# Seven products for eight in the gate projection, expert rows added onto the output by accumulating DMAs, deferred semaphore clears, and a sixth weight buffer

## The chip, the cores and the metric

One core of a Trainium2 chip. The metric is device time in microseconds of one execution of the whole kernel. The kernel before takes 1611.61 us, the median of three runs (1611.59 to 1613.59).

## The reference

One layer of a decoder block, 1024 tokens of width 1024, float32. A modulated RMSNorm of x, then one input projection whose columns feed an RWKV-7 time mixing, a latent attention, and two gates of 1024 channels each; the two branches are projected to 1024, weighted by the gates, summed, projected again and added to x. Then a second RMSNorm and a mixture of 32 experts, two per token:

```
h = modulate(rmsnorm(x, g_norm_mix), sh_m, sc_m)
z = h @ w_in                                  # z_rwkv, z_mla, z_gates (2 x 1024 columns)
gate_rwkv, gate_mla = split(sigmoid(z_gates))
x = x + gt_m * ((gate_rwkv * (y_rwkv @ w_branch[0]) + gate_mla * (y_mla @ w_branch[1])) @ w_out)
h = modulate(rmsnorm(x, g_norm_ffn), sh_f, sc_f)
for e in range(32):                           # combine[:, e] is 0 for all but two experts of a token
    out += combine[:, e] * ((silu(h @ w_e_gate[e]) * (h @ w_e_up[e])) @ w_e_down[e])
return x + gt_f * out
```

## The kernel before

Each engine runs its own program, written out by hand with semaphore waits; nothing is scheduled by a planner. The work is in five phases: norms and the latent projections, the low-rank parts of the time mixing, the time mixing itself, attention, and the last one, which holds the gates, the branch projections, the output projection, routing and the experts. `phase()` (L225) ends each with a block of its own in which GpSimd clears all semaphores of the phase one by one (L234), with a barrier of all engines behind it.

**Products in two parts.** A float32 product of full accuracy is made of three float32r matmuls (`three`, L341): every operand is split into a high part (ACT, `high_part`, L335) and a low part (DVE, `low_part`, L338), and high x high, high x low and low x high are summed in PSUM.

**Gates (L2118 to L2135).** A tile is 128 gate channels x 1024 tokens: 8 slices of K x 2 halves of the tokens x 3 matmuls of 512 columns = 48 matmuls. There are 16 tiles, 8 for each of the two gates, in a loop of the engines over i with both gates `br` in its body. SyncE loads the next weights (0.5 MB) when a tile's matmuls are done, ACT takes the sigmoid of a finished tile out of PSUM into `G` and splits the next weights, DVE makes their low part. The h of both operands lies split in `hs`; the first splits of h and of the weights are made in the attention phase (`SPLITS`, L1813).

**Branches and output (L2137 to L2197).** y of the time mixing is read back into `x1[:, 0:4]` and split while the gates run. y of the attention lies in `YTM` and is split only after the last gate tile, since its high part goes over the split h (ACT L2221, DVE L2276 into `v_lo7`). The branch tile of `b` has the 24 matmuls of the first branch, then the 24 of the second.

**Routing (L2655 to L2748).** DVE finds each token's two experts and their weights `top`, and builds one-hot tiles; 16 matmuls (L2509) turn them into `idx`, the token of each row of each pass, and `home`, the row number 0 to 2047 (token + 1024 for a token's second expert) to which the result goes.

**Experts (L2412 to L2653).** 24 fixed passes of 128 rows, 96 rows of room per expert, so 4 experts in 3 passes; then a loop over overflow passes. Per pass, GpSimd gathers the rows of h by an indirect DMA into one of three buffers `xg` (`fetch`), TensorE transposes them (L2520), multiplies by gate and up weights (L2542) and by the down weights (L2560); DVE multiplies the result by the FFN gate `gt` into one of four buffers `yo` (`rows_out`, L2768), and GpSimd sends these 128 rows by an indirect DMA to `y_dram`, 2048 rows (`send`, L2457). Unused rows carry an index out of bounds and move nothing. SyncE loads the experts' weights, 3 MB each, into five buffers: expert e goes out when the pass that last used expert e - 5 is through. GpSimd's order in the loop (L2468): wait for a free `xg`, gather, wait for `yo` of an earlier pass, send.

**Tail (L2782 to L2802).** When all sends have landed, SyncE reads the 2048 rows back in 16 DMAs, DVE adds each times `top` onto `x1` (L2789), and SyncE stores the 8 tiles of the output.

Of the kernel before, what the change touches and what calls it, by code (L numbers as in the profile page):

```python
# [15 lines left out]
P = 128  # L16
D = 1024
SEQ = 1024
KD = D // P
# [24 lines left out]
WB = 5  # L44
# [135 lines left out]
def build(nc, x, c, w_ada, b_ada, g_norm_mix, g_norm_ffn, w_decay_up, w_a_up, w_g_up, g_q_a, w_uq, g_kv_a,  # L180
# [6 lines left out]
    yr_dram = nc.dram_tensor("rwkv_rows", (P, CT * SEQ), f32, kind="Internal").ap()  # L187
    h2_dram = nc.dram_tensor("h2_rows", (SEQ, D), f32, kind="Internal").ap()
    y_dram = nc.dram_tensor("expert_rows", (2 * SEQ, D), f32, kind="Internal").ap()
    ctx = ExitStack()  # L190
    with ctx:
# [3 lines left out]
        taken = []  # L195
# [4 lines left out]
        r_in = [ctx.enter_context(nc.semaphore(f"r_in{i}")) for i in range(2 * NT)]  # L200
        w_in7 = [ctx.enter_context(nc.semaphore(f"w_in7{i}")) for i in range(2)]
        h_in7 = [ctx.enter_context(nc.semaphore(f"h_in7{i}")) for i in range(KD // PIECE)]
        mod_out = ctx.enter_context(nc.semaphore("mod_out"))
# [11 lines left out]
        def sem(st, name):  # L215
            taken.append(st.enter_context(nc.semaphore(name)))
            return taken[-1]
# [680 lines left out]
        with phase() as st:  # L898
# [14 lines left out]
            with nc.Block() as block:  # L913
# [11 lines left out]
                def _(pool):  # L925
                    nc.gpsimd.tensor_copy(crep2, csig[:].unsqueeze(2).broadcast_to([P, KD, 32])).then_inc(rep2_s, 1)
                    nc.gpsimd.memset(lw_pad[:, CT * SEQ:], 0.0)

# [91 lines left out]
        with phase() as st:  # L1020
# [91 lines left out]
            with nc.Block() as block:  # L1112
# [15 lines left out]
                def _(pool):  # L1128
# [53 lines left out]
                    for j in PERIODS:  # L1182
# [14 lines left out]
                        if step(n):  # L1197
                            inner_blocks(n)
                            outer_blocks(n, 0)

# [601 lines left out]
        with ExitStack() as st:  # L1802
            sb(st, "x1_place", [P, NT, D])
            sb(st, "G_place", [P, 2, KD, SEQ])
            hs = alias("hs", [P, 2, KD, SEQ])
            hraw = sb(st, "hraw", [P, 2, KD, SEQ])
            wh = alias("wh7", [P, 2, 1024])
            sb(st, "gt7_place", [P, 2, 1024])
            wl = alias("wl7", [P, 2, 1024])
            wraw = sb(st, "wraw7", [P, 2, 1024])  # L1810
        hh, hl = hs[:, 0], hs[:, 1]
        KLATE = 3
        SPLITS = [None, None] + list(range(KLATE, KD))  # L1813
# [3 lines left out]
        def gate_weights(sp, i, br):  # L1817
            src = w_gates[bass.ds(i + br * KD, 1)].rearrange("a p k n -> (a p) (k n)")
            sp.dma_start(wraw[:, br], src).then_inc(w_in7[br], 16)
# [1002 lines left out]
```

## Time and profile before

| what | value |
|---|---|
| median of 3 runs | 1611.61 us |
| profiled execution, its own time | 1609.88 us |
| its span, first to last instruction | 1608.0 us |
| mean granted TensorE clock | 0.941 of 2.4 GHz |
| TensorE matmuls busy | 1410.4 us, 14393 instructions |
| DVE / ACT / GpSimd busy | 700.8 / 470.3 / 258.6 us |
| moved by DMA | 238.07 MB |
| gate stage (from the first gate matmul to the first branch matmul) | 829 to 1004.5 us |
| expert passes (first gathered rows to the last send) | 1254.7 to 1568 us |
| tail (reading back, weighting, storing, clears) | 1568 to 1608 us |

The spans of the stages are read from the start times of their first and last instructions. Matmuls overlap: one of 512 columns is listed with 0.39 us, while the next one starts 0.225 us after it, so work on TensorE is counted by the pitch of the starts.

### The profile page before, as it was taken

To read this page: it belongs to the slowest core of one execution; us is meant where nothing else is said; L and a number is where in the kernel's file an instruction comes from. 1 tells how busy PE (TensorE), PEld (TensorE's weight loads), DVE (VectorE), ACT (ScalarE), POOL (GpSimd) and SP (SyncE) were. 2 spreads that over 40 slices of the span, in tenths; PEclk is the share of its full clock that TensorE was granted. 3 is DMA by queue.
4 is the path that set the end of the run, shared out by engine and by line. 5 is a ranking of instruction groups with operands and counts; after the bars stand their busy time and mean duration, and the time that the engine had idled before them with its cause. 6 is when DMAs were issued, how large, how long until landed. Compare 5 with 4: busy or idle time off the path is not lost. (4 is left out here: it accounts for less than half of the span.)

```text
span 1608.0 us, 32972 instructions
## 1 busy us (share of the span) xinstructions
PE 1410.4 (88%) x14393; PEld 1014.7 (63%) x14393; DVE 700.8 (44%) x990; ACT 470.3 (29%) x839; POOL 258.6 (16%) x301
## 2 busy tenths in 40 slices
PE   3799999965999988799889999998994899999980
PEld 0587777724899987577678888786883433333320
DVE  0645776746676755444641101555435212112124
ACT  1543232252343443444542222222111111111110
POOL 0001221205565551011110000000000111111110
PEclk8899999987999999799999999999996799999995
DMA  9831222260000020730011111313118599999947
GB/s 358 301 116 53 84 75 65 73 250 2 4 4 4 4 62 30 192 123 2 1 63 43 52 52 39 147 49 148 40 40 342 206 354 418 416 416 402 399 182 313
DMA packets 78759, 238.07 MB, mean 148 GB/s; under 512 B 8473, under 2 KB 41753, under 8 KB 61985
## 3 DMA queue, kind: packets, MB, share of 16 engines
q1 hardware_dynamic: 71280, 219.30, 36.9%
q0 software_dynamic: 7344, 16.79, 2.8%
q8 instruction: 108, 1.77, 0.4%
q14 instruction: 27, 0.21, 0.0%
HBM read 209.82 MB, written 36.19 MB: 153 GB/s over the span
## 5 line engine op out<-in xcount | busy, mean ns | idle before, releaser
L2542 PE MATMUL ps<-gu,xT 128*32 128x512 f32 x1536 | 176.5, 601 | 2.6 <-DMA gu<-w_e_up 2.0
L343 PE MATMUL ps<-hs,wh 128*128 128x512 f32 x320 | 125.9, 393 | 6.2 <-DVE v_lo L339 3.7
L345 PE MATMUL ps<-hs,wl 128*128 128x512 f32 x320 | 126.2, 394 | 0.0
L2542 PEld LDWEIGHTS ps<-gu,xT 128*32 128x32 f32 x1536 | 48.1, 111 | 108.3 <-issue 104.3
L2757 DVE TENSOR_TENSOR sg<-sg,ps 128x256 f32<-128x256 f32 x25 | 10.5, 422 | 213.4 <-ACT sg L2628 213.4
L344 PE MATMUL ps<-hs,wh 128*128 128x512 f32 x256 | 100.3, 392 | 0.0
L339 DVE TENSOR_TENSOR wl<-wraw,wh 128x1024 fp32r<-128x1024 f32 x24 | 29.4, 1225 | 150.5 <-ACT wh L336 150.5
L343 PE MATMUL ps<-hh,wr_h 128*128 128x512 f32 x224 | 93.1, 416 | 0.6 <-DVE wr_l L339 0.6
L344 PE MATMUL ps<-hl,wr_h 128*128 128x512 f32 x224 | 88.5, 395 | 0.0
L345 PE MATMUL ps<-hh,wr_l 128*128 128x512 f32 x224 | 88.4, 395 | 0.0
L2560 PE MATMUL ps<-dn,hidT 128*32 128x512 f32 x768 | 86.8, 592 | 0.5 <-ACT hidT L2632 0.5
L1996 DVE TENSOR_REDUCE nmax<-ps 128x1 f32<-128x896 f32 (+4 forms) x64 | 45.9, 753 | 71.7 <-PE ps L1895 71.1
L1392 DVE TENSOR_TENSOR inverses<-inverses,ps 128x512 f32<-128x512 f32 (+1 forms) x80 | 49.9, 631 | 61.5 <-PE ps L1615 61.1
L1178 POOL TENSOR_TENSOR off<-mats,cst 128x256 f32<-128x256 f32 x80 | 66.1, 845 | 53.4 <-PE ps L1599 53.3
L343 PEld LDWEIGHTS ps<-hs,wh 128*128 128x128 f32 x320 | 61.0, 191 | 20.0 <-DVE v_lo L339 4.1
L1615 PE MATMUL ps<-inverses,xx 64*64 64x64 f32 x1280 | 71.5, 218 | 0.2
L1890 PE MATMUL ps<-kT,qT 96*128 96x512 f32 (+3 forms) x160 | 63.6, 505 | 6.9 <-ACT causalr L1977 6.9
L345 PEld LDWEIGHTS ps<-hs,wl 128*128 128x128 f32 x320 | 60.9, 190 | 12.9
L2463 POOL MEMSET xg<- 128x3072 f32 x1 | 2.7, 2659 | 392.9 <-DVE YTM L2338 392.9
L1615 PEld LDWEIGHTS ps<-inverses,xx 64*64 64x64 f32 x1280 | 63.6, 135 | 0.4 <-issue 0.3
L1612 PE MATMUL ps<-xx,inverses 64*64 64x64 f32 x1024 | 63.3, 220 | 0.1
L487 POOL TENSOR_TENSOR qk<-qk,g_row 128x768 f32<-128x768 f32 x16 | 37.7, 2380 | 154.8 <-DVE qk L739 154.8
(366 smaller groups left out, 3018.5 us busy)
## 6 DMA issues: line engine op xcount, KB each, us to landing
gu<-w_e_gate SPq DMA_DIRECT2D x34, 1024.0 KB, 12.8
gu<-w_e_up SPq DMA_DIRECT2D x34, 1024.0 KB, 14.8
dn<-w_e_down SPq DMA_DIRECT2D x34, 1024.0 KB
wbuf<-w_ada SPq DMA_DIRECT2D x16, 1024.0 KB, 11.3
wbuf<-w_ada SPq DMA_DIRECT2D x16, 512.0 KB, 5.5
wraw<-w_gates SPq DMA_DIRECT2D x16, 512.0 KB, 3.3
rows<-expert_rows SPq DMA_DIRECT2D x16, 512.0 KB, 10.0
wr<-w_rwkv SPq DMA_DIRECT2D x14, 512.0 KB, 3.6
```

The source lines that it names most:

```text
L343: nc.tensor.matmul(out, wt[0], mov[0], start=(k == 0), stop=False)
L344: nc.tensor.matmul(out, wt[0], mov[1], start=False, stop=False)
L345: return nc.tensor.matmul(out, wt[1], mov[0], start=False, stop=(k == kn - 1))
L487: nc.gpsimd.tensor_tensor(rows, rows, g_row[:, i].unsqueeze(1).broadcast_to([P, HEADS, QKD]), ALU.mult).then_inc(gained, 1)
L1178: nc.gpsimd.tensor_tensor(off[:, g], mats[:, n % 2, 4 * g:4 * g + 4, 0], cst[:, a:a + CHUNK].unsqueeze(1).broadcast_to([P, 4, CHUNK]), ALU ...
L1392: nc.vector.tensor_tensor(now, now, add, ALU.add).then_inc(sm["t_ev"], 1)
L1612: nc.tensor.matmul(o[rows, 0:CHUNK], tt(j)[rows, hh, 1], xx[rows, hh], start=True, stop=True)
L1615: m = nc.tensor.matmul(o[rows, CHUNK:], xx[rows, hh], tt(j)[rows, hh, 1], start=True, stop=True)
L1890: nc.tensor.matmul(ps[:, 2 * (u % 2) + at // 512, at % 512:at % 512 + to - at], q, kT_[:, at - o * P:to - o * P], start=True, stop=True)
L1996: nc.vector.tensor_reduce(nmax[:, n:n + 1], score(u, i, o), AX.X, ALU.max, negate=True)\
L2542: last = nc.tensor.matmul(ps[part, GB[b]], xT[:, b, k, part], gu[:, expert(m, c_) % WB, :, k], start=(k == 0), stop=(k == KD - 1))
L2560: last = nc.tensor.matmul(ps[part, 6 + half], hidT[:, b, k, part], dn[:, expert(m, c_) % WB, k, half * 512:(half + 1) * 512], start=(k == ...
```

## The change

All four parts are in one diff.

**Clears.** The semaphores of a phase are held until the next phase is over, and GpSimd clears them there, in the middle of its own order. The block with its barrier is gone. Those of the last phase aren't cleared.

```diff
+        def clear_signals_of_last_phase(pool):
+            for s_ in before:
+                pool.sem_clear(s_)
...
             with ExitStack() as st:
                 yield st
-                with nc.Block() as block:
-                    @block.gpsimd
-                    def _(pool):
-                        for s_ in taken:
-                            pool.sem_clear(s_)
-                taken.clear()
+            held[1].close()
+            held.reverse()
+            before[:] = here
+            here.clear()
```

**Gates.** The tile i = 0 of both gates is made as before. For i = 1 to 7 the two tiles (2 x 128 channels by 1024 tokens, K = 1024) are taken as a 2 x 2 by 2 x 2 block product and made with seven block products (Strassen's scheme in Winograd's form). Each is 4 slices of K x 3 matmuls of 512 columns. The sums of h are made once at the start (T1, T2, T3 and one in place, 128x2048 each), the sums of the weights for each i. Products P1, P6, P7, P4 add up in one PSUM bank, out of which ACT copies the state after each of the first three; DVE adds the other banks. Loops of the engines over i are written out.

```diff
+            FACTORS = (A11, A21, S2, A12, S3, S4, A22)
+            P1, P5, P6, P2, P7, P3, P4 = range(7)
+            BANK = (0, 2, 0, 1, 0, 3, 0)
...
+                def product(i, j):
+                    pe.wait_ge(w_lo, number(i, j) + 2)
+                    if i == 1 and j in (P5, P6, P7, P4):
+                        pe.wait_ge(t_lo, (P5, P6, P7, P4).index(j) + 1)
+                    if j == P1 and i >= 2:
+                        pe.wait_ge(g_ev, evacuated(i - 2))
+                    if j in (P6, P7, P4):
+                        pe.wait_ge(ev_a, 3 * (i - 1) + (P6, P7, P4).index(j) + 1)
...
+                    for k in range(CT):
+                        cols = slice(k * P, (k + 1) * P)
+                        nc.tensor.matmul(out_t, hi[:, cols], mov_hi[:, k], start=(fresh and k == 0), stop=False,
+                                         skip_group_check=True)
+                        nc.tensor.matmul(out_t, hi[:, cols], mov_lo[:, k], start=False, stop=False,
+                                         skip_group_check=True)
+                        m = nc.tensor.matmul(out_t, lo[:, cols], mov_hi[:, k], start=False, stop=(k == CT - 1),
+                                             skip_group_check=True)
```

ACT splits product j's factor once product j - 2 is done (two buffers for high parts). The order of DVE within a step:

```diff
+                for i in range(1, KD):
+                    last = i == KD - 1
+                    if i > 1:
+                        factor_low(i, P5)
+                    factor_low(i, P6)
+                    factor_low(i, P2)
+                    if i == 1:
+                        sum_low(3)
+                    add(i, 0)
+                    factor_low(i, P7)
+                    add(i, 1)
+                    factor_low(i, P3)
+                    if last:
+                        y_low(0)
+                        y_low(1)
+                    factor_low(i, P4)
+                    add(i, 2)
+                    if last:
+                        y_low(2)
+                        y_low(3)
+                        weights(0, 7 * (KD - 1) + 2)
+                    else:
+                        for which in (SUM3, SUM1, SUM2):
+                            sums(i + 1, which)
+                        factor_low(i + 1, P1)
+                        sums(i + 1, SUM4)
+                    add(i, 3)
```

The sums need room: h is loaded a second time (4 MB) at the start of the phase, y of the time mixing is read back late, y of the attention is stored (2 MB) and read back. Both are split in four pieces each. The first branch products of both `b` now come before the second branch's, which alone wait for `v_lo`.

**Experts.** The routing matmuls carry a second half of columns (`block_is` has the token and its share, 84 columns for 42), which gives the share of each row; `home` is held twice, as it is and less 1024. The output tiles x1 are stored to `out` as they are made. Each pass's rows are multiplied by their share and the gate in one DVE operation, and are added onto `out` by two DMAs, one for the rows that are their token's first expert and one for the others; each waits until the one before it has landed.

```diff
+                def add(col, buf, done):
                     pool.indirect_dma_start(
-                        out=y_dram, out_offset=bass.IndirectOffsetOnAxis(ap=col.bitcast(u32), axis=0),
+                        out=out[0], out_offset=bass.IndirectOffsetOnAxis(ap=col.bitcast(u32), axis=0),
                         in_=yo[:, buf], in_offset=None,
-                        bounds_check=2 * SEQ - 1, oob_is_err=False).then_inc(y_out[buf], 16)
+                        bounds_check=SEQ - 1, oob_is_err=False, compute_op=ALU.add).then_inc(done, 16)
+
+                def add_first(j):
+                    pool.wait_ge(y_ev, 2 * j + 2)
+                    if j:
+                        pool.wait_ge(second_out, 16 * j)
...
+                    add(home[:, j, 0:1], j % YSLOTS, first_out)
+
+                def add_second(j):
+                    pool.wait_ge(first_out, 16 * j + 16)
+                    add(home[:, j, 1:2], j % YSLOTS, second_out)
...
                     fetch(idx[:, m:m + 1], m % XSLOTS)
-                    if m == XSLOTS:
-                        pool.wait_ge(home_s, 1)
-                    if m >= XSLOTS + 2:
-                        j = m - XSLOTS - 2
-                        pool.wait_ge(y_ev, 2 * j + 2)
-                        send(home[:, j:j + 1], j % YSLOTS)
+                    j = m - XSLOTS - 2
+                    if j >= 1:
+                        add_second(j - 1)
+                    if j >= 0:
+                        add_first(j)
...
-                        nc.vector.tensor_tensor(yo[:, buf, cols], ps[:, 6 + half], gt[:, cols], ALU.mult)\
-                          .then_inc(y_ev, 1)
+                        nc.vector.scalar_tensor_tensor(yo[:, buf, cols], ps[:, 6 + half], share_, gt[:, cols],
+                                                       ALU.mult, ALU.mult).then_inc(y_ev, 1)
+
+                def fixed_rows_out(m):
+                    if m >= YSLOTS:
+                        dve.wait_ge(second_out, 16 * (m - YSLOTS + 1))
+                    rows_out(m, m % YSLOTS, share[:, m:m + 1])
```

The tail (both blocks from L2782 to L2802) is gone. **WB = 6**: the sixth weight buffer and the FFN gate lie in the room of x1, so SyncE waits for the stores of x1 before it loads expert 5; it then goes out with experts 1 to 4, before the first pass.

## Rows read from the trace of the kernel before

**Rows 1.** The page: span, busy time by engine, GpSimd's DMA queue

```profile
span 1608.0 us, 32972 instructions
PE 1410.4 (88%) x14393; PEld 1014.7 (63%) x14393; DVE 700.8 (44%) x990; ACT 470.3 (29%) x839; POOL 258.6 (16%) x301
...
q0 software_dynamic: 7344, 16.79, 2.8%
```

**Rows 2.** Windows of four stages: length, busy by engine, clock, DMA share, GB/s

```profile
core 0: us, PE busy (x) PEld busy (x) DVE busy (x) ACT busy (x) POOL busy (x), PEclk, DMA share, GB/s
866.00:904.00 38.00, 38.00 (x169) 31.49 (x168) 4.90 (x4) 8.61 (x8) 0.00 (x0) 1.00 0.13 43
...
1222.00:1252.00 30.00, 12.51 (x53) 11.21 (x52) 21.79 (x60) 2.32 (x4) 0.91 (x1) 0.50 1.01 419
...
1344.00:1500.00 156.00, 154.05 (x1390) 55.35 (x1386) 28.96 (x53) 24.11 (x52) 26.40 (x26) 1.00 1.01 411
...
1568.00:1603.00 35.00, 0.00 (x0) 0.00 (x0) 20.01 (x16) 0.00 (x0) 0.00 (x0) 0.50 0.91 360
```

**Rows 3.** Chain of waits, routing and experts: start us, length us, what

```profile
1254.67 4.50 DMA xg<-h_rows,idx
...
1276.48 0.90 PE ps L2520 x8
...
1346.08 20.82 DMA gu<-w_e_up
...
1537.97 0.89 PE ps L2520 x8
```

**Rows 4.** Groups by shape in the gate stage, 830 to 1004 us, DVE and ACT

```profile
L339 DVE TENSOR_TENSOR wl<-wraw,wh 128x1024 fp32r<-128x1024 f32 x15 | 18.4, 1226 | 135.6 <-ACT wh L336 135.6
L339 DVE TENSOR_TENSOR yr<-x,yr 128x4096 fp32r<-128x4096 f32 x1 | 4.4, 4426 | 7.7 <-ACT yr L336 7.7
...
L2213 ACT ACTIVATE G<-ps 128x1024 f32 x14 | 14.4, 1028 | 45.2 <-PE ps L345 45.1
```

**Rows 5.** Waits, 828 to 1014 us: total, times, longest

```profile
PE ps L343 <- DVE v_lo L339: 3.7, 1, 3.7
```

**Rows 6.** Groups by shape in the expert stage, 1284 to 1500 us, DVE and ACT

```profile
L2768 DVE TENSOR_TENSOR YTM<-ps,gt 128x512 f32<-128x512 f32 x37 | 25.6, 692 | 27.1 <-PE ps L2560 27.1
...
L2623 ACT ACTIVATE xT<-ps 128x512 f32<-128x512 f32 x36 | 19.6, 595 | 2.2
```

**Rows 7.** Line L234, whole span, then 325 to 340, then from 1600 us

```profile
L234 POOLq EVENT_SEMAPHORE_RANGE_CLEAR  x244: 37/38/47, 329.1 to 1607.3; - x122
...
L234 POOLq EVENT_SEMAPHORE_RANGE_CLEAR  x79: 37/38/47, 329.1 to 334.5; - x79
...
L234 POOLq EVENT_SEMAPHORE_RANGE_CLEAR  x73: 37/38/43, 1602.7 to 1607.3; - x73
```

**Rows 8.** Chain of waits, last expert rows and tail

```profile
1563.87 0.70 DVE YTM L2768
1564.70 0.50 issue
1565.43 2.61 DMA expert_rows<-YTM,now
...
1592.80 1.28 DVE x L2789
```

**Rows 9.** Groups by shape in routing, 1230 to 1256 us

```profile
L2509 PE MATMUL ps<-block_is,row_is 128*128 128x42 f32 x32 | 7.1, 420 | 7.9 <-DVE row_is L2731 7.9
...
L2501 PE MATMUL ps<-each,rt 128*128 128x256 f32 x2 | 1.2, 715 | 8.9 <-DVE each L2690 8.9
...
L2729 DVE SCALAR_TENSOR_TENSOR block_is<-rt,block_is 128x336 f32<-128x336 f32 x2 | 1.0, 508 | 0.1
```

**Rows 10.** Line L2458: 1286 to 1516 us, then 1547 to 1549, then 1565 to 1567

```profile
L2458 POOL DMA_INDIRECT expert_rows<-YTM,home x20: 1002/1011/1016, 1286.0 to 1512.1; - x20
...
DMA to landing us min/median/max: 8.4/9.1/10.1
...
DMA to landing us min/median/max: 4.1/4.1/4.1
...
DMA to landing us min/median/max: 2.6/2.6/2.6
```

More of the change, by code:

```diff
@@ L193, in sb @@
             return st.enter_context(nc.sbuf_tensor(name, shape, dt))
-        taken = []
+        here, before = [], []
+        held = [ctx.enter_context(ExitStack()) for _ in range(2)]
         gu_in = [ctx.enter_context(nc.semaphore(f"gu_in{i}")) for i in range(WB)]
@@ new lines, in _, with branch_part @@
+                for br in range(2):
+                    whole_gate(br)
+                for i in range(1, KD):
+                    for j in range(7):
+                        product(i, j)
+                def branch_part(i, b, br):
+                    mov = ((yh, yl), (None, v_lo7))[br]
+                    for n in range(2):
+                        at = slice(n * 512, (n + 1) * 512)
+                        for k in range(CT):
+                            cols = slice((br * CT + k) * P, (br * CT + k + 1) * P)
+                            high = vh(k)[:, n] if br else mov[0][:, k, at]
+                            m = three(ps[:, 4 * b + 2 * br + n], (wh[:, b, cols], wl[:, b, cols]), (high, mov[1][:, k, at]),
+                                      k, CT)
+                    m.then_inc(b_mm, 1)
@@ L2218, in _, with factor_high @@
-                for br in range(2):
-                    gate(KD - 1, br)
-                    if br:
-                        high_part(vh, YTM[:]).then_inc(v_hi, 1)
-                    weights(br, KD * 16 + 16)
+                def factor_high(i, j):
+                    act.wait_ge(g_mm, max(1, 1 + number(i, j)))
+                    sums = {P5: SUM1, P6: SUM2, P7: SUM3, P3: SUM4}
+                    if j in sums:
+                        act.wait_ge(s_sum, 4 * (i - 1) + sums[j])
+                    else:
+                        act.wait_ge(w_in7[i % 2][FACTORS[j][0]], 16 * (i // 2 + 1))
+                    high_part(factor_hi(i, j), factor(i, j)).then_inc(w_hi, 1)
@@ L2224, in merged @@
+                gates(KD - 1)
+                weights(1, KD * 8 + 16)
+                for k in range(CT):
+                    v_high(k)
                 def merged(i):
@@ new lines, in y_low, with v_low @@
+                def y_low(k):
+                    dve.wait_ge(y_hi, k + 1)
+                    low_part(yl[:, k], x1[:, k], yh[:, k]).then_inc(y_lo, 1)
+                def v_low(k):
+                    dve.wait_ge(v_hi, k + 1)
+                    low_part(in_halves(v_lo7[:, k]), in_halves(YTM[:, k]), vh(k)).then_inc(v_lo, 1)
+                for which in (SUM3, SUM1, SUM2, SUM4):
+                    sums(1, which)
+                dve.wait_ge(raw_in[0], 16)
+                nc.vector.tensor_tensor(T1[:, 0], h12, h11, ALU.subtract).then_inc(t_sum, 1)
@@ L2280, in merge @@
+                weights(1, 7 * (KD - 1) + 3)
+                for k in range(CT):
+                    v_low(k)
+                def merge(i, b, ready=None):
                     m = 2 * i + b
@@ L2572, in gate_up @@
                             part = slice(UNIT * b, UNIT * (b + 1))
[L2573 removed]
+                            last = nc.tensor.matmul(ps[part, GB[0]], xT[:, 0, k, part], gu[OVER_W[b]][:, :, k],
                                                     start=(k == 0), stop=(k == KD - 1))
```

489 lines of the change are left out of this document (321 added, 168 removed).

## The prediction

> **What bounds the kernel now.** I read the page first: in 1608.0 us of span TensorE is busy 1410.4, DVE 700.8, and GpSimd's DMA queue carries 16.8 MB, half of it gathered rows and half sent ones [rows 1]. Then the windows by stage [rows 2]. In the gate stage, 866 to 904 us, TensorE is full at clock 1.00 (2.4 GHz) with 169 matmuls in 38 us, so one every 0.225 us; DVE does 4.9 of the 38, DMA is at 0.13. In the expert stage, 1344 to 1500, TensorE is busy 154 of 156 us and the DMA share is 1.01 at 411 GB/s: two resources are full at once. From 1568 to 1603 TensorE does nothing and the DMA engines move 360 GB/s: the tail. The chain of waits [rows 3] says the same: transposes of one expert pass follow the last by 11.76 us at best, from 1276.48 to 1537.97 are 22 passes in 261.5 us, 11.89 each, and in between stand a few pieces of "DMA gu<-w_e_up" that waited in a queue for 20 us. So any matmul less in the gate stage counts in full, everything after 1568 counts in full, and in the expert stage nothing may be slowed that sits on the DMA engines.
>
> **Part 1, seven products for eight.** The 16 gate tiles have 48 matmuls each. The first two stay; in each of the seven steps behind them 96 become 7 x 12 = 84. 7 x 12 matmuls less at 0.225 us [rows 2] = 18.9 us off TensorE. What is new: per step DVE has 4 sums, 7 low parts and 4 additions out of PSUM, each 128x512. The nearest row is 0.69 us for 128x512 out of PSUM [rows 6]: 15 x 0.69 = 10.4 us. ACT has 7 high parts, 3 copies at 0.60 each [rows 6] and 2048 columns of sigmoids, 1.03 per 1024 [rows 4]: 8.1 us. A step is 84 x 0.225 = 18.9 us, so both fit as sums. The order is tighter: from the end of P7 to the next step's P1 TensorE has two products, 5.4 us, while ACT copies and splits (1.2) and DVE has six operations in a row (low part of P4, addition, three sums, low part of P1: 4.1) with hand-overs of 0.3: 5.6. That is 0.2 us per step, 1.5 in all. At the start DVE must do four low parts of 1024 columns, six operations of 512, and seven of 2048 (1.23 us per 1024 [rows 4]; 4.43 for 4096 gives 2.2 to 2.45): 4.9 + 4.1 + 16.3 = 25.3 us, and waits some 2 us for the new loads, before it can split P6's factor; TensorE is there after 96 + 24 matmuls, 27 us. DVE starts a microsecond later than TensorE, so P6 comes 3.7 us late (bounds 0 and 8). At the end TensorE now waits 3.7 us for v_lo [rows 5]; with the second branch in pieces and 48 matmuls (10.8 us) ahead of it, this goes, but the pieces of y are in ACT's and DVE's order ahead of the first branch weights: four high and low parts plus one split after P7, some 1.7 us late. Part 1: -18.9 + 1.5 + 3.7 - 3.7 + 1.7 = -15.7 us.
> The added transfers (4 MB of h at the start, 4 MB of reloads, 2 MB stored) fall where the DMA share is 0.13 [rows 2]; their cover is some 20 us of matmuls each.
>
> **Part 2, the clears.** GpSimd clears 244 semaphores one by one, 73 of them after the last transfer [rows 7]. They take 0.065 us each (1602.7 to 1607.3 for the last 73) and every engine waits at a barrier: 244 x 0.065 = 15.9 us. They move into GpSimd's order beside other work (171 are left, the longest lot 79, 5.1 us, in stages where GpSimd has hardly any work) and the last 73 vanish. With them go five barriers; from the last clear, 1607.3, to the end of the span there are 0.7 us [rows 1, 7], and with one of two barriers left I take 0.3 us each, an estimate. -17.4 us.
>
> **Part 3, the tail.** Now the last send lands at 1565.43 + 2.61 = 1568.0 [rows 8], then 16 reads, 16 additions of 1.28 and 8 stores follow, up to 1602.7, where the clears begin [rows 7]. All of it goes: -34.7 us. The stores of x1 move into the output stage, one of 0.5 MB per tile of rows; nothing waits for them but SyncE, ahead of the sixth buffer.
>
> **Part 4, routing and first rows.** Two DVE operations of 336 elements (0.51 each) come ahead of the matmuls of L2509, and these have 84 columns for 42: +1.0 and, between 0 and 1.9 (42 more columns at the 1.4 ns per column between 0.42 us for 42 and 0.71 for 256 [rows 9]), I take +1.0. With the sixth buffer SyncE queues experts 1 to 5 and two stores, 16.8 MB, from 1221.5 on; at 419 GB/s [rows 2] that ends at 1261.6, where it ended at 1252. The first gather took 4.50 us beside little else [rows 3]; issued behind queued weights GpSimd's DMAs take 8.4 or more [rows 10]. Queue half gone by then: +3 us. Part 4: +5 us.
>
> **Part 5, the accumulating DMAs.** This decides the sign. For each pass the one send becomes two additions into the output, and no addition may start before the last has landed. The trace has no such DMA; the nearest rows are the sends. While weights stream, 20 sends land after 8.4 to 10.1 us, median 9.1; without weights one took 4.1 and the small last one 2.6 [rows 10]. From DVE's end to the DMA's start there are 0.86 us (1564.57 to 1565.43 [rows 8]). An addition carries half of a pass's rows, so I take the low end under load, 8.4 + 0.8 = 9.2, and without weights 3.2, between 2.6 and 4.1, + 0.8 = 4.0. Two under load make 18.4 us per pass against 11.89: the chain of additions becomes what sets the pace, and with four output buffers DVE and TensorE soon wait for it. That in turn leaves the DMA engines idle at times, where additions are fast. The account over the stage: from the first rows out (1285) 27 experts of 3.15 MB and 7 of the 8.4 MB of gathered rows remain, 92 MB; at 411 GB/s [rows 2] 224 us, and 10 more for the additions' own bytes in that time: 234 us under load. In these fit 234 / 9.2 = 25.4 additions; the other 22.6 take 4.0 each, 90 us. Chain: 324 us, from 1285.1 to 1609.4. Behind it the overflow pass: copies on GpSimd, two products with the gate on DVE (1.4), two additions of 2.6 + 0.86, in all some 9.5 us: 1618.8 in place of 1568.0, **+50.8 us**. The bounds: +3.5 (the additions stay within 11.89 us per pass and only the last pass has a second one, 0.86 + 2.6), and 48 x 9.9 = 475 us, which is +202.
> The waits ahead of each addition stand in GpSimd's order ahead of the next gather; three gather buffers and four output buffers cover that until the chain is the pace, and then the gather is early. The sixth buffer itself removes at most the 2 us by which TensorE waits for weights; beside a slower pace it is worth nothing.
> An addition reads the row it changes. If that doubles its bytes, 42 rows or 0.17 MB per DMA, 0.42 us, come on top: 48 x 0.42 + 6 = 26 us more. The Trainium skill (Collectives: The Full Stack, "The bandwidth ceiling: the fold count and why AG ≠ RS ≠ AR") says exactly this: an add in the DMA path needs two source reads on one ring and so runs at half a copy's rate. By that rule the sum would be 1626; no run here shows it yet, and I hold the copy's price because the landing under load hardly is a matter of bytes (the same 9 us for all 20 sends).
>
> **Sum.** 1608.0 - 15.7 - 17.4 - 34.7 + 5.0 + 50.8 = 1596.0 us of span; the profiled execution is 1.9 above its span, 1609.88, so 1597.9. The median of the runs is 1611.61, 1.7 above that execution: **1600 us**, 0.7% faster.
>
> **Rivals.**
> A, the forecast, 1600, own range 1580 to 1622. For it: landings of 9 us with the DMA engines full. Chance 0.40.
> B, the additions hide: two of them within a pass, a mean of 5.9 us or less with hand-over. Then 1600 - 50.8 + 3.5 = 1553. For it: an addition has half the rows, and sends of 4 us exist. Against: all 20 beside weights took 8.4 or more. Chance 0.22.
> C, slower: the chain of additions at the GpSimd queue is the pace all through, at a mean of 8 us per addition: 48 x 8 = 384, 60 us more than A, 1660. It decides against the change from a mean of 7.0 us on (336 us of chain eat all that parts 1 to 4 bring); A has 6.75, so the point is near. Chance 0.16.
> D, the seven products save nothing, because ACT's and DVE's order keeps TensorE waiting at each product: 1616. Each product has 2.7 us, and a split needs 1.4 to 2.3 of them. Chance 0.10.
> E, the row read as well as written counts double: 1626. Chance 0.12.
>
> **How the numbers follow.** A measurement of this kernel can tell 0.2%, 3.2 us, from no change, so faster means below 1608.4. A gives 0.30 faster, 0.04 same, 0.06 slower; B 0.22 faster; C 0.16 slower; D 0.04, 0.03, 0.03; E 0.01, 0.02, 0.09. Sum: 0.57, 0.09, 0.34. The range takes in B's 1553 and most of C: 1545 to 1655.
>
> **What would show it.** Part 1: gate steps of about 19 us, TensorE waits on DVE near their start only. Part 2: no stop of all engines for 79 clears at 329 [rows 7]. Part 3: no TensorE-free stretch of 35 us. Part 5: in the expert stage, transposes 13 to 14 us apart in place of 11.76, GpSimd and DVE waiting for the additions' landings, a DMA share well under 1, additions landing after 8 to 9 us beside weights and 3 to 4 alone. It is wrong if the passes keep 11.8 us (B), or if additions take over 8 us even where the DMA share is low (C).

## The result, and the profile after

The changed kernel takes 1695.47 us (median of 4 runs, 1690.71 to 1698.15) beside 1612.6 us for the kernel before on the same chip: ratio 1.0513, interval 1.0487 to 1.0539, so 5.1% slower. The forecast was 1600 us, range 1545 to 1655. The side is wrong and the time lies outside the range. It came out on the side of rival C (slower, the chain of additions as the pace), 35 us above C's 1660. The profiled execution took 1693.2 us, 1.9 of it outside its span.

The page of the changed kernel:

```profile
span 1691.3 us, 32837 instructions
PE 1418.3 (84%) x14309; PEld 1006.0 (59%) x14309; DVE 752.1 (44%) x1083; ACT 496.9 (29%) x906; POOL 312.5 (18%) x327
...
q0 software_dynamic: 10944, 16.82, 4.7%
...
DMA 23%; PE 22%; DVE 3%; issue 2%; ACT 1%; SPq 0%; POOLq 0%; POOL 0%; DVEq 0%
...
L2729 POOL DMA_INDIRECT out<-YTM,home x48 | 75.1, 1565 | 301.8 <-DMA out<-YTM,home 228.2
```

Against [rows 1] the span is 83.3 us longer. TensorE has 84 matmuls fewer, and 273.0 us of the span without work where it had 197.6. Just under a quarter of the chain that ended last is DMA, and the last row says whose: GpSimd issued 48 additions and waited 228 us for the landing of the one before. GpSimd's queue carries the same 16.8 MB as before, but its packets took 4.7% of the engines' time in place of 2.8%.

Windows of the changed kernel by stage (columns as in [rows 2]):

```profile
core 0: us, PE busy (x) PEld busy (x) DVE busy (x) ACT busy (x) POOL busy (x), PEclk, DMA share, GB/s
855.00:985.00 130.00, 130.00 (x563) 106.56 (x561) 68.12 (x102) 55.73 (x89) 0.00 (x0) 0.99 0.22 76
1280.00:1340.00 60.00, 59.93 (x540) 21.52 (x532) 11.72 (x20) 9.30 (x21) 11.06 (x8) 1.00 0.97 372
1340.00:1500.00 160.00, 117.22 (x928) 41.46 (x932) 20.60 (x36) 17.28 (x36) 37.80 (x27) 0.84 0.80 285
...
1600.00:1660.00 60.00, 27.48 (x216) 8.78 (x208) 6.95 (x12) 3.00 (x7) 18.17 (x12) 0.75 0.19 27
```

The gate stage is full with the seven products, at half of DVE's and under half of ACT's time. The expert stage is the new thing. Up to 1340 TensorE is full: four output buffers still hold what the additions have not taken away. From 1340 to 1500 it is busy 117 of 160 us, the DMA share is 0.80 where it was 1.01 [rows 2], and neither resource is the bound any more. From 1600 to 1660 no weights are left to load (27 GB/s). TensorE is full there up to 1628; then its work is done but for the overflow pass's last products, and it stands 40.5 us, until 1668.5, while the last additions go out one by one.

The chain of waits of the changed kernel (start us, length us, what):

```profile
1231.25 8.98 DMA xg<-h_rows,idx
...
1266.30 0.82 issue
1267.12 10.08 DMA out<-YTM,home
...
1277.25 0.76 issue
1278.01 9.88 DMA out<-YTM,home
...
1658.43 4.38 DMA out<-YTM,home
...
1666.22 2.20 DMA xg<-h_rows,now
...
1671.68 5.06 PE ps L2878 x16
...
1678.39 4.50 DMA out<-YTM,now
```

From 1267.12 on the pattern is landing, hand-over, landing, hand-over (the hand-over is the time from a landing to the start of the next addition). The first piece answers to the 4.50 us gather of [rows 3]. The last ones belong to the overflow pass. The gather that starts only at 1666.22 brings the rows of the block behind it; their transposes stand in TensorE's order ahead of the overflow pass's down product (5.06 us).

Line L2729 of the changed kernel, the additions, first over the whole span, then from 1267 to 1345 us (weights streaming), then from 1610 to 1660 us (none left):

```profile
L2729 POOL DMA_INDIRECT out<-YTM,home x48: 1551/1552/1609, 1267.1 to 1663.6; - x48
...
L2729 POOL DMA_INDIRECT out<-YTM,home x8: 1551/1579/1609, 1267.1 to 1343.1; - x8
...
DMA to landing us min/median/max: 8.9/10.0/10.8
...
L2729 POOL DMA_INDIRECT out<-YTM,home x9: 1551/1552/1552, 1613.1 to 1658.4; - x9
...
DMA to landing us min/median/max: 3.9/4.6/5.4
```

The last two groups hold the two prices that the forecast had to guess. It took 8.4 and 3.2 us; they are 10.0 and 4.6. Issuing one costs GpSimd 1.55 us where a send cost 1.01 [rows 10].

Waits from 1231 to 1691 us (total, times, longest):

```profile
POOL out L2729 <- DMA out<-YTM,home: 228.2, 39, 9.7
...
PE ps L2812 <- DMA xg<-h_rows,idx: 80.0, 11, 10.7
POOL out L2729 <- DVE YTM L3062: 70.7, 8, 10.4
...
PE ps L2812 <- DMA xg<-h_rows,now: 40.5, 1, 40.5
```

Two of these need care. TensorE waits 80 us for gathered rows, which looks like slow gathers; it is a symptom, because a gather is issued by GpSimd and stands in its order behind an addition that waits for a landing (experiments 5 and 6 settle that). And the 70.7 us that GpSimd waited "for DVE": 17.0 us of them are true: the first addition (7.0) and the first of the overflow pass (10.0) had only DVE's rows to wait for. The other six are not. In the chain such an addition starts 0.04 us after the end of DVE's operation, 0.83 us after the last landing. All 47 additions of the fixed passes behind the first follow the last landing by 0.76 to 0.87 us, but for two (1.14 and 1.55), so the landing held these too; the two events nearly coincide, since DVE was itself held up by the buffer that this landing set free.

**The time, stretch by stretch.** Kernels with the same program up to the first gather issue it anywhere from 1227.2 to 1237.0 us in their profiles, so single positions are good to a few microseconds; I compare durations. From the first matmul of the gate stage to the first gather: 412.3 us (818.91 to 1231.25), before 425.8 (828.89 to 1254.67). A little of this difference belongs to the clears: in the first 5.1 us of the stretch the kernel before has a granted clock of 0.67 and 15 matmuls, the changed kernel 1.00 and 22, and with the clears alone moved (experiment 1) the clock is 1.00 there too. From the gather to the first rows out: 35.9 us, before 31.3. From there to the end of the span: 424.2 us, before 322.0, and in those 322.0 the tail and the last clears (40.0 us) were included. So the whole loss, and more, lies behind the first rows out.

### The profile page after: what moved, and what is told of

Its sections match the earlier page's. It is cut to its first block, busy times and chain, and to the rows that moved or that the text cites. A ratio compares the mean times of both kernels' runs of the same rounds, so it can differ in the third digit from the quotient of the medians.

```text
span 1691.3 us, 32837 instructions
## 1 busy us (share of the span) xinstructions
PE 1418.3 (84%) x14309; PEld 1006.0 (59%) x14309; DVE 752.1 (44%) x1083; ACT 496.9 (29%) x906; POOL 312.5 (18%) x327
## 3 DMA queue, kind: packets, MB, share of 16 engines
q0 software_dynamic: 10944, 16.82, 4.7%
HBM read 207.73 MB, written 51.40 MB: 153 GB/s over the span
## 4 chain that ended last, share of the span: by engine, by line
DMA 23%; PE 22%; DVE 3%; issue 2%; ACT 1%; SPq 0%; POOLq 0%; POOL 0%; DVEq 0%
DMA out<-YTM,home 21%; PE ps L350 3%; PE ps L351 3%; PE ps L352 3%; PE ps L2229 3%; PE ps L2231 3%; PE ps L2233 3%; PE ps L2834 1%; DMA br<-b_router 1%; PE ps L2284 1%; PE ps L2275 1%; DMA xg<-h_rows,idx 1%; PE ps L2800 0%; PE ps L2812 0%; DVE YTM L3062 0%
## 5 line engine op out<-in xcount | busy, mean ns | idle before, releaser
L2834 PE MATMUL ps<-gu,xT 128*32 128x512 f32 x1296 | 188.8, 637 | 0.7 <-ACT xT L2915 0.7
L3053 DVE TENSOR_TENSOR sg<-sg,ps 128x256 f32<-128x256 f32 x25 | 10.5, 422 | 297.4 <-ACT sg L2920 297.4
L2812 PE MATMUL ps<-cst,xg 128*128 128x128 f32 x208 | 37.9, 341 | 120.5 <-DMA xg<-h_rows,idx 80.0
L2729 POOL DMA_INDIRECT out<-YTM,home x48 | 75.1, 1565 | 301.8 <-DMA out<-YTM,home 228.2
L2812 PEld LDWEIGHTS ps<-cst,xg 128*128 128x128 f32 x208 | 32.1, 205 | 124.4 <-DMA xg<-h_rows,idx 82.1
L2915 ACT ACTIVATE xT<-ps 128x512 f32<-128x512 f32 x52 | 29.4, 596 | 160.8 <-PE ps L2812 159.4
L2834 PE MATMUL ps<-gu_last,xT 128*32 128x512 f32 x240 | 62.6, 635 | 0.0
L350 PE MATMUL ps<-hs,M 128*128 128x512 f32 x144 | 57.9, 402 | 1.6 <-DVE hs L346 1.6
## 6 DMA issues: line engine op xcount, KB each, us to landing
gu<-w_e_gate SPq DMA_DIRECT2D x29, 1024.0 KB, 10.5
```

The costliest lines, as they stand in the source:

```text
L350: nc.tensor.matmul(out, wt[0], mov[0], start=(k == 0), stop=False)
L2729: pool.indirect_dma_start(out=out[0], out_offset=bass.IndirectOffsetOnAxis(ap=col.bitcast(u32), axis=0), in_=yo[:, buf], in_offset=None, b ...
L2812: last = nc.tensor.transpose(ps[:, g, j * P:(j + 1) * P], rows[:, 4 * g + j], C("ident"))
L2834: last = nc.tensor.matmul(ps[part, GB[b]], xT[:, b, k, part], gu[expert(m, c_) % WB][:, :, k], start=(k == 0), stop=(k == KD - 1))
```

## Experiments

Experiments 3 to 6 are one run each, all others medians of four; experiment 6 was run four times more as the last of 9 to 11.

**1. The clears alone.** The kernel before, with each stage's semaphores cleared by GpSimd inside a later stage:

```
-                with nc.Block() as block:
-                    @block.gpsimd
-                    def _(pool):
-                        for s_ in taken:
-                            pool.sem_clear(s_)
-                taken.clear()
+            held[1].close()
+            held.reverse()
+            before[:] = here
+            here.clear()
...
+                    clear_signals_of_last_phase(pool)
```

> The kernel before with the deferred clears alone. If all engines wait for the 244 clears and the barriers behind them, it saves 17.4 us: 1595 us. If other work (a transfer, a first load of the next phase) ends just as late, it saves less, 8 to 12 us: 1601 to 1605.

Measured: 1591.0 us against 1610.38, ratio 0.9891 (0.9867 to 0.9915). That is 19.4 us less; the forecast's part 2 was 17.4. Its span is 1588.9.

**2. Clears and seven products.** The same with the gate and branch part of the change; experts, sends, five weight buffers and the tail as before:

```
-        wh = alias("wh7", [P, 2, 1024])
+        small_r = alias("small_r", [P, 5, 512])
...
+        FACTORS = (A11, A21, S2, A12, S3, S4, A22)
+        P1, P5, P6, P2, P7, P3, P4 = range(7)
...
+                def product(i, j):
```

> The kernel before with the clears and the seven products, experts, sends, five buffers and tail as before. With 13.6 us for the seven products (18.9 less matmuls, 5 of waits at the start and at the end) on top of 17.4 for the clears: 1581 to 1583 us. If ACT's and DVE's order holds TensorE up at each product, no better than the clears alone: 1595.

Measured: 1575.31 us, ratio 0.979 (0.9774 to 0.9806), 15.7 us below experiment 1. Part 1 had said 15.7; for this run I had expected 13.6 and 1581 to 1583, and it lies below that. The agreement with part 1 to the tenth is luck: the four runs of this kernel lie between 1572.62 and 1578.00 us, those of experiment 1 between 1589.37 and 1596.80. The wait for P6's split is 7.3 us here and 6.6 in the changed kernel, where I had 3.7; against that, of the waits that I had put within the steps and at the end of the stage (1.5 and 1.7 us) TensorE has 0.5 us here and 1.0 in the changed kernel. This kernel computes all of the reference and beats both kernels of the case. Its expert stage shows what a full one looks like (window, columns as above):

```profile
1340.00:1500.00 160.00, 159.15 (x1436) 57.55 (x1432) 28.95 (x52) 25.90 (x56) 25.37 (x25) 1.00 1.00 408
```

So 1575 to 1695, 120 us, is what the new way out of the expert stage costs, with the shares in the routing and the sixth buffer in it (118 us by the two ratios, since the two kernels ran on different chips), though it saves the tail of 34.7 us.

**3. The same DMAs without the addition.** The changed kernel; the two DMAs of a pass overwrite rows of the output in place of adding to them, in the same order with the same waits:

```
                         in_=yo[:, buf], in_offset=None,
-                        bounds_check=SEQ - 1, oob_is_err=False, compute_op=ALU.add).then_inc(done, 16)
+                        bounds_check=SEQ - 1, oob_is_err=False).then_inc(done, 16)
```

> The changed kernel with the two DMAs of a pass as plain copies onto the output, everything waiting as before (leaves out the addition, so rows hold one expert's share alone). If the cost is the order (each DMA waits for the landing of the last), it stays far above the kernel before: 48 landings, each shorter by the 0.55 us of issue and perhaps 0.5 for the row that isn't read, 1640 to 1670 us. If the cost is the adding, it falls to 1600 or less.

Measured: 1622.17 us, below the 1640 to 1670 that I expected. Line L2729 of this kernel over the span, then from 1267 to 1345 and from 1565 to 1600 us:

```profile
L2729 POOL DMA_INDIRECT out<-YTM,home x48: 977/987/1009, 1267.7 to 1594.0; - x48
...
DMA to landing us min/median/max: 3.8/8.3/9.4
...
DMA to landing us min/median/max: 2.4/2.7/3.3
```

And the DMA queue on its page:

```profile
q0 software_dynamic: 10944, 16.80, 2.9%
```

Start to start is (1594.0 - 1267.7) / 47 = 6.94 us per DMA; my account, made from sends, had 324 / 48 = 6.75. The account was sound for copies. With the addition it is (1663.6 - 1267.1) / 47 = 8.44. So adding costs 1.5 us per DMA, 70 us over 47 steps, of the 71.0 us between the spans (1691.3 and 1620.3). The two windows show it as +1.7 us beside weights and +1.9 alone, 0.57 of it in the issue. The queue's row shows the same from the engines' side: the same 10944 packets took 2.9% of 1620.3 us here and 4.7% of 1691.3 there, so 1.7 times the engine time. The gathers are in both, so for the additions alone the factor is higher. An estimate: with 24 additions fewer (experiment 6) the queue takes 3.0% of 1551.5 us; by the difference 48 additions take some 66 us of engine time and the gathers 13.5, which leaves 33.5 for the 48 copies: a factor of about 2.

The order alone is dear too: even with copies the kernel stays at 1622, above the kernel before. And for copies the low end of my prices was right: 8.3 us beside weights for my 8.4, and 2.7 alone for my 3.2.

**4. The same additions without the weight stream.** The changed kernel; of the weights of 26 of the 32 experts only an eighth is loaded, so their products use stale weights (the loads of the down weights are cut in the same way):

```
+                        if e < WB:
+                            sp.dma_start(gu[e % WB][:, half], view[:, e]).then_inc(gu_in[e % WB], 16)
+                        else:
+                            sp.dma_start(gu[e % WB][:, half, 0], view[:, e, 0]).then_inc(gu_in[e % WB], 16)
```

> The changed kernel with 26 of 32 experts' weight loads cut to a sliver each (leaves out most of the weights, so these experts compute with others' weights). If an addition costs 4.9 us of landing without weights beside it and 0.8 of hand-over, 48 take 272 us, less than 24 passes of TensorE at 11.76, and the stage runs at about TensorE's pace: 1585 to 1605 us in all, landings of 4 to 5.5. If an addition is slow by itself, landings stay at 8 or more and the time above 1660. If the stage is held by gathers standing behind GpSimd's waits, TensorE still waits some 80 us for gathered rows.

Measured: 1585.41 us. The additions over the whole span, and a window:

```profile
L2735 POOL DMA_INDIRECT out<-YTM,home x48: 1551/1552/1608, 1263.1 to 1555.1; - x48
...
DMA to landing us min/median/max: 3.9/5.2/10.3
```

```profile
1340.00:1500.00 160.00, 160.00 (x1446) 56.97 (x1438) 32.81 (x56) 24.46 (x53) 52.67 (x38) 1.00 0.50 112
```

The time lies at the lower end of what I expected. With the weights cut, 112 GB/s are left and a DMA share of 0.50. The landing falls from 10.0 to 5.2 us and the time from start to start to (1555.1 - 1263.1) / 47 = 6.21 us, 12.4 per pass: a little over a pass, so that the output buffers hold the difference and TensorE stays full. TensorE's waits for gathered rows of the fixed passes are gone but for the first gather's (10.9 us), though the gathers' order was not touched. The rest of the weight stream thus costs 8.44 - 6.21 = 2.2 us per addition.

**5. No order between the additions.** The changed kernel; both additions of a pass go out at once, the second onto another array, and neither waits for another's landing. The second rows are left out of the output:

```
-                    add(home[:, j, 0:1], j % YSLOTS, first_out)
-
-                def add_second(j):
-                    pool.wait_ge(first_out, 16 * j + 16)
-                    add(home[:, j, 1:2], j % YSLOTS, second_out)
+                    add(home[:, j, 0:1], j % YSLOTS)
+                    place(home[:, j, 1:2], j % YSLOTS)
```

> The changed kernel with both additions of a pass issued at once, the second onto another array, neither waiting for an earlier pass (leaves out adding the second experts' rows to the output). Number, kind and bytes of the DMAs stay. If the cost is the order, passes go back to TensorE's pace, 11.8 to 12.2 us, and the time to 1543 to 1560 us, with landings of 9 us and more that nobody waits for. If the cost is the additions' load on the DMA engines or on GpSimd, passes stay above 13 us and the time above 1600.

Measured: 1570.88 us, span 1569.0: 122 us below the changed kernel with as many accumulating DMAs, so the order is the cost. But I had expected 1543 to 1560. A window and the longest pieces of the chain point to the cause:

```profile
1340.00:1500.00 160.00, 152.79 (x1348) 53.73 (x1344) 30.48 (x52) 22.65 (x49) 54.58 (x39) 0.97 1.02 386
```

```profile
1394.14 26.91 DMA gu<-w_e_up
...
1472.19 25.31 DMA gu_last<-w_e_up
```

The DMA engines are full (1.02) and move 386 GB/s where experiment 2 moved 408 at a share of 1.00. In this window GpSimd's queue takes 22.9% of the engines' time and the queue of the weights 78.7%; in experiment 6 it is 15.1% and 86.1%. The additions take engine time from the weights, and TensorE loses 7 us in this window to late weights. That the additions' load alone makes the rest of the 18 us to the next experiment was not tried apart.

**6. One ordered addition per pass.** The changed kernel without the second additions, the first still in strict order; the second rows are left out of the output:

```
-                    add(home[:, j, 0:1], j % YSLOTS, first_out)
+                    add(home[:, j, 0:1], j % YSLOTS, second_out)
 
                 def add_second(j):
-                    pool.wait_ge(first_out, 16 * j + 16)
-                    add(home[:, j, 1:2], j % YSLOTS, second_out)
+                    pass
```

> The changed kernel with the first addition of each pass alone, each still waiting for the one before (leaves out the rows of the second experts). If the order costs one landing and one hand-over per DMA, 9.9 + 0.8 us beside weights is less than a pass of 11.8 and is hidden: 1545 to 1560 us. If the second DMA is not the point and any ordered addition slows the stage: above 1600.

Measured: 1553.29 us. Line and window:

```profile
L2729 POOL DMA_INDIRECT out<-YTM,home x24: 1552/1587/1608, 1267.0 to 1532.0; - x24
...
DMA to landing us min/median/max: 4.4/9.6/11.4
```

```profile
1340.00:1500.00 160.00, 160.00 (x1445) 57.54 (x1447) 32.07 (x55) 25.79 (x56) 34.17 (x26) 1.00 1.02 400
```

And TensorE's wait for gathered rows, from the waits from 1225 us to the end (total, times, longest):

```profile
PE ps L2810 <- DMA xg<-h_rows,idx: 10.8, 1, 10.8
```

A landing of 9.6 us with hand-over is 10.4, less than a pass: the order is kept and TensorE stays full, start to start is (1532.0 - 1267.0) / 23 = 11.5 us. The step from here to 16.9 us per pass comes from the second landing in the same pass; that two landings don't fit into a pass and one does decides the case. The one wait for gathered rows is that for the first gather; the changed kernel has 11, 80.0 us in all. The weight stream is whole here and in experiment 5 (10.9 us, once), so those 80 us, but for the first gather's 10.7, came from the order of the additions and not from slow gathers.

**7. A complete kernel without the long order.** The first rows are added onto the output, the second ones copied to an array of their own without waits between them, and a tail reads that array and adds it in eight accumulating DMAs:

```
+                for t in range(NT):
+                    sp.dma_start(rows[:, t], y2_dram[t * P:(t + 1) * P]).then_inc(r_in[t], 16)
...
+                    pool.wait_ge(r_in[t], 16)
+                    pool.dma_start(out_v[t], rows[:, t], accum_op=ALU.add).then_inc(o_out, 16)
```

> A full kernel: first experts' rows are added onto the output, second experts' rows are copied to an array of 1024 rows, neither waits for an earlier pass; behind the last pass the second rows are read and added onto the output in eight accumulating DMAs. 20 to 30 us more than the unchained one for its tail of 4 MB read and 4 MB added: 1565 to 1580 us. If additions that run beside the weights slow them (each addition reads 4 KB more per row), the passes are 12.3 us and more and it is 1585 or above.

Measured: 1593.75 us, ratio 0.9889 (0.9873 to 0.9906); above the 1565 to 1580 that I expected. The passes did what they should. Expert stage, then tail:

```profile
1340.00:1500.00 160.00, 159.73 (x1440) 57.71 (x1436) 31.22 (x53) 25.54 (x55) 50.21 (x41) 1.00 1.02 404
...
1550.00:1595.00 45.00, 0.00 (x0) 0.00 (x0) 0.00 (x0) 0.00 (x0) 9.14 (x10) 0.53 0.75 188
```

The tail is 45 us without TensorE for 4 MB read and 4 MB added, where the tail of before did twice the reads, the additions on DVE and the stores in 35 us at 360 GB/s [rows 2]. Here the engines are busy at 0.75 and move 188 GB/s. Large accumulating DMAs are no bargain either.

**8. The missed wait.** The changed kernel; the gather of the overflow pass's next rows is issued ahead of the last fixed pass's additions in place of behind all of them:

```
                     add_first(j)
+                    if j == FIXED - 2:
+                        pool.wait_ge(xt_s, 2 * FIXED + 2)
+                        fetch(idx[:, FIXED + 1:FIXED + 2], 0)
                 add_second(FIXED - 1)
```

> The changed kernel with the gather of the row block behind the overflow pass issued before the last fixed pass's additions. TensorE waits 40.5 us for this gather, with the overflow pass's down product behind it. If it is on the path, 9 to 13 us less, 1682 to 1686. If the chain of additions hides it, no change: 1695.

Measured: 1684.75 us, ratio 1.0449 (1.0424 to 1.0473), 10.7 us less. The chain of waits behind the last fixed addition:

```profile
1665.53 4.29 DMA out<-YTM,home
...
1670.10 0.12 POOL now_share L2779
...
1670.50 0.06 DVE YTM L3066
...
1672.79 4.59 DMA out<-YTM,now
```

From the last fixed landing (1669.82) to the first overflow addition there are now 3.0 us; in the changed kernel it was 10.5 (1663.57 + 4.3 = 1667.9 to 1678.39). Gather, transposes and products now run beside the chain and no longer after it. These 7.5 us are shown; what made the other 3 of the 10.7 was not looked for, and the four runs of this kernel lie 7.7 us apart.

**9. to 11. The sixth buffer.** Three kernels on one chip: the changed kernel with five weight buffers, and experiment 6 with five and with six.

```
-WB = 6
+WB = 5
```

> The changed kernel with five weight buffers in place of six. The chain of additions is the pace, so the buffer itself gives nothing; without it expert 5 isn't in the queue ahead of the first gather, which lands after 4.5 us in place of 9.0: 3 to 5 us less, 1690 to 1692. If the sixth buffer keeps the passes going, it is slower than 1695.

> The kernel first_only (one addition per pass, second rows left out) with five weight buffers. Here TensorE is the pace. First gather 4.5 us earlier, against that the 2 us of waits for weights that the kernel before has: 1549 to 1553 us beside first_only_six. If the sixth buffer is worth something where TensorE is the pace, 5 us or more slower than first_only_six.

> The kernel first_only once more, timed in rounds, as the other side of the comparison of buffers: 1553 us as in its first look.

Measured: 1692.69 us (ratio 1.0512, 1.0472 to 1.0553) for the changed kernel with five; 1551.36 (0.9636, 0.9607 to 0.9664) and 1552.31 (0.9641, 0.962 to 0.9663) for experiment 6 with five and with six. The sixth buffer is worth nothing that can be measured, neither beside the slow chain nor where TensorE is full. It has a price all the same: with five buffers the first gather lands after 5.07 and 4.74 us, with six after 8.98 and, in the last of the three, 9.18. That price doesn't show in the times, which lie 1 us apart in experiment 6.

## Why the prediction was wrong

**The step that failed** is the price in part 5: "I take the low end under load, 8.4 + 0.8 = 9.2, and without weights 3.2". An accumulating DMA was priced as a plain send. Measured are 10.0 and 4.6 us, mean start to start 8.44 against 6.75. The low end itself, taken because an addition moves fewer rows, was no error: experiment 3 holds everything but the adding, lands after 8.3 and 2.7 us and comes to 6.94 from start to start. The mechanism was right as I put it: the order of landings sets the pace, the buffers fill, the DMA share falls; only the passes are 16.9 us apart where I had 13 to 14. It is the forecast's own mechanism at a higher price, and C only by its mean (8 us) and its side: C's sign, additions over 8 us even where the DMA share is low, did not come (4.6 us). From the first start to the last landing the chain took 400.8 us (1267.12 to 1667.9) for 324: +77. I had named the deciding point, a mean of 7.0 us, seen that I stood 0.25 us from it, and still gave the far side 0.16 (0.28 with E). With a guessed price so near its deciding point the two sides deserved near equal chances; and both errors of the price pointed the same way, since the change adds work to the DMA that was my nearest row.

**A second step was missing.** "Behind it the overflow pass: ... in all some 9.5 us". From the last fixed landing to the end there were 23.4 us, 13.9 more. In GpSimd's order the gather of the rows behind that pass stands behind the last additions, and behind that gather stand transposes and, in TensorE's order, the pass's down product of 5.06 us; experiment 8 takes them from behind the chain: 7.5 us there, 10.7 in all. The two overflow additions at 4.5 and 4.2 us in place of 2.6 make 3.5 more. And the span runs on for 3.4 us after the last landing (1683.74 + 4.2 = 1687.9), which the forecast had left out. I had written that gathers stand behind the additions, and that the gather would be early once the chain is the pace. The gather was early in neither place: in the fixed passes TensorE waits ten times for gathered rows behind an addition (69.3 us, the 80.0 less the first gather's 10.7), which costs nothing there because the chain goes on without a gap, and at the loop's end the late gather is a part of the chain itself.

**E, the doubled read**, was the right suspicion with the wrong size: 0.42 us per DMA by bytes, 1.5 measured. The Trainium skill (Collectives: The Full Stack, "The bandwidth ceiling: the fold count and why AG ≠ RS ≠ AR") has a reduce at half a copy's rate because of its two source reads; the engine time agrees as far as it can be read here, 1.7 times the copies' for the whole queue and, by the estimate in experiment 3, about 2 for the additions alone. But a rate is not what bounds a DMA of some 43 rows: alone it lands after 4.6 us where a copy takes 2.7, and the price to take was one per DMA. The Trainium skill (DMA: Bandwidth & Descriptors, "Anatomy of one DMA — SWDGE (gpsimd) path") gives a fixed part of some 2.0 us plus bytes at 436 GB/s, by which my estimate for 0.17 MB is 2.4 us. The copies alone agree (2.7); the additions (4.6) do not, and nothing in that formula gives the 8.3 and 10.0 us beside a weight stream.

**B**, the additions hidden, would have needed 5.9 us per addition. Not even experiment 4, with most of the weight stream gone, is that fast (6.21), so B is out for this kernel with its two landings per pass. **D** is out: 15.7 us saved.

**What held.**
- Part 1: 15.7 forecast, 15.7 measured (experiment 2 less experiment 1). P6's wait was too small in the forecast (3.7 for 6.6), the total still right, which is luck (experiment 2). The 3.7 doesn't even follow from the forecast's own terms: 25.3 + 2 + 1 less 27 is 1.3. In the trace DVE waits 4.2 us for the loads of h where I had 2, and 2.0 us for ACT's high part of the last sum, which the forecast had not. From the first gate matmul to the first gather the changed kernel saves 13.4 us; parts 1 and 4 gave 15.7 - 2.0 = 13.7 for that stretch.
- Part 2: 17.4 forecast, 19.4 measured.
- Part 3: the reads, additions and stores of the tail are gone as said. But the sign that I had given for it, no stretch of 35 us without TensorE, did not come: TensorE stands 40.5 us at the end, now for the chain of additions.
- Part 4: the first gather took 4.5 us longer (8.98 for 4.50), forecast 3; with five buffers it takes 5.07, so the loads of expert 5 ahead of it are the cause.
- The sixth buffer: at most 2 us forecast, nothing measured.
- The hand-over: 0.8 us forecast, 0.76 to 0.87 measured.

**The sum by the measured terms.** Forecast span 1596.0. The first addition starts 3.9 us later than the forecast's 1263.2 (1285.96 less 15.7, less the 12.1 us of clears that lie ahead of it, 17.4 less the last 5.3, plus 5), the chain adds 77.4 (400.8 less the 323.4 between that start and the last landing), and the end 13.9. That is 1691.2, against 1691.3 measured. The three stretches are cut out of the measured span, so their sum had to come out; what it tells is how the 95 us are shared.

**What stays open.** Why a landing beside the weight stream takes 8 to 10 us for copies and additions alike was not taken apart. It hangs on that stream: 10.0 us with it, 5.2 with most of it gone (experiment 4). The Trainium skill (DMA: Bandwidth & Descriptors, "Latency and other measured facts") has the completion of a DMA grow with the load on the memory; the direction agrees, and its figures, 0.2 us on average and 2 us at high load, are smaller than the step seen here.

## What to carry to other kernels

DMAs that must each wait for the landing of the last form a chain with its own pace: landing plus hand-over, times their number per pass. Compare that with the pass before anything else; one landing of 10 us in a pass of 11.8 was free here, a second cost 5 us in every pass and made the kernel 5% slower, although the change saved 15.7, 19.4 and 34.7 us elsewhere. Price an accumulating DMA above a copy (here 1.5 us each, plus load on the DMA engines), never like a copy; and where an engine's instructions wait for such a chain, read what stands behind them in its order at the end of the loop as well as inside.

## What the runs showed of the hardware

- Adding in an indirect DMA of some 43 rows: issue 1.55 us for the copy's 0.99, landing alone 4.6 for 2.7, beside weights 10.0 for 8.3. The byte counts of the profile's page do not show the read of the target rows (207.73 MB read with and without the addition); the packets' share of engine time does (4.7% for 2.9%, gathers included).
- The engines can be busy and move little: eight large accumulating DMAs with their reads kept them at 0.75 with 188 GB/s (experiment 7).
- Positions in single profiles: kernels with the same program up to the first gather issue it between 1227.2 and 1237.0 us. A difference of a few microseconds has to be read between two marks of one trace, or from medians of several runs.
- TensorE came back from the 6.6 us wait in the gate stage at the lower of its two levels, 1.2 GHz. The first two matmuls behind the wait, from the timeline of the changed kernel (start us, length us):

```profile
853.88 0.80 PE L2229 MATMUL ps<-tr,small_r 128*128 128x512 f32 x1 [6.58 <-DVE small_r L346]
854.47 0.63 PE L2231 MATMUL ps<-tr,small_r 128*128 128x512 f32 x1
```

They come 0.43 us apart up to 858.7, and the granted clock of that stretch is 0.50; from 859 on it is 1.00 and they come 0.23 apart. With twelve matmuls at the lower level the wait of 6.6 us costs some 9. The forecast had left that out.
